# Feed-forward block: the tokens' norm factor behind its first products; attention's first maxima beside the last chain; the queries' weights ahead of the tables

## The reference, cut to what matters

```python
# end of the first block
x = x + y                               # y: the mixed heads times dn_w_out
x = x + squared_relu_mlp(rms_norm(x, norm_mlp[i]), mlp_w_up[i], mlp_w_down[i])
def squared_relu_mlp(h, w_up, w_down):  # D = 1024, D_FF = 4096
    return jnp.square(jax.nn.relu(h @ w_up)) @ w_down
def rms_norm(x, w):                     # y * w, with y = x * rsqrt(mean(x * x) + eps)
...
# second block, attention
qx = apply_rope(rmsnorm(heads(px[0], ATT_HEADS, ATT_HEAD_DIM), g_q[l]), cos, sin)
kx = apply_rope(rmsnorm(heads(px[1], ATT_KV_HEADS, ATT_HEAD_DIM), g_k[l]), cos, sin)
s = jnp.einsum('bqkgd,bnkd->bkgqn', q, keys).astype(jnp.float32) * scale
p = jax.nn.softmax(s, axis=-1)
```

## Time and profile before

| | |
|---|---|
| median of 3 runs | 3222.49 us (3222.05 to 3223.61) |
| profiled execution: time, span | 3223.74 us, 3222.0 us |
| PE busy | 3057.1 us, 95% of the span |
| DVE, ACT, POOL busy | 1556.7, 997.9, 450.8 us |
| mean granted clock of TensorE | 0.982 |
| chain that ended last, PE's share | 85% |

### The profile page before, as it was taken

One profiled execution on the slowest core, in us unless ns is written; L12 is line 12 of the kernel. 1 busy time (PEld: TensorE's weight loads), 2 busy tenths in 40 slices (PEclk: granted clock), 3 DMA queues, 4 the chain that ended last, 5 costly groups with the idle time before them and its releaser, 6 DMA issues.

```text
span 3222.0 us, 36124 instructions
## 1 busy us (share of the span) xinstructions
PE 3057.1 (95%) x14927; PEld 2493.4 (77%) x14927; DVE 1556.7 (48%) x1915; ACT 997.9 (31%) x1440; POOL 450.8 (14%) x352
## 2 busy tenths in 40 slices
PE   7899999989899999999979999999998999999997
PEld 5688888878688888888765667888876888888886
DVE  7566666653565553433456773466654222222224
ACT  5555555552211122212333332233232211111111
POOL 4333333321000001001300000233310000000001
PEclk9999999999999999999989999999999999999999
DMA  3111111122133431111220001011131111111111
GB/s 123 40 47 47 46 47 46 47 66 98 59 118 118 128 117 57 47 52 46 92 54 5 9 9 44 20 40 34 53 107 31 52 53 46 46 52 46 46 46 59
DMA packets 77236, 184.76 MB, mean 57 GB/s; under 512 B 7056, under 2 KB 29072, under 8 KB 77072
## 3 DMA queue, kind: packets, MB, share of 16 engines
q1 hardware_dynamic: 77072, 182.44, 17.9%
HBM read 163.87 MB, written 15.79 MB: 56 GB/s over the span
## 4 chain that ended last, share of the span: by engine, by line
PE 85%; DVE 8%; ACT 4%; issue 2%; DMA 0%; POOL 0%; SPq 0%; POOLq 0%; DVEq 0%; ACTq 0%
PE ps L512 38%; PE ps L1561 18%; PE ps L2886 9%; PE ps L2227 4%; DVE b L2835 2%; PE ps L2365 1%; PE ps L2195 1%; PE ps L909 1%; PE ps L2220 1%; PE ps L2219 1%; DVE b L501 1%; ACT b L493 1%; PE ps L916 1%; PE ps L86 1%; PE ps L891 1%
## 5 line engine op out<-in xcount | busy, mean ns | idle before, releaser
L512 PE MATMUL ps<-b 128*128 128x512 f32 x6024 | 1498.5, 400 | 40.1 <-DVE b L501 13.6
L512 PEld LDWEIGHTS ps<-b 128*128 128x128 f32 x6024 | 1111.2, 190 | 258.2 <-issue 19.2
L1561 PE MATMUL ps<-b 128*128 128x512 f32 x2592 | 599.1, 392 | 0.7 <-DVE b L1696 0.7
L1561 PEld LDWEIGHTS ps<-b 128*128 128x128 f32 x2592 | 485.1, 188 | 109.2 <-DVE b L1696 1.1
L501 DVE TENSOR_TENSOR b<-b 128x1024 fp32r<-128x1024 f32 (+1 forms) x206 | 255.4, 1241 | 298.8 <-ACT b L493 291.9
L493 ACT ACTIVATE b<-b 128x1024 fp32r<-128x1024 f32 (+1 forms) x206 | 215.1, 1045 | 524.5 <-PE ps L1561 427.6
L2886 PE MATMUL ps<-b 128*128 128x512 f32 (+1 forms) x1464 | 330.1, 381 | 6.8 <-ACT b L2946 5.9
L2886 PEld LDWEIGHTS ps<-b 128*128 128x128 f32 x1464 | 257.1, 193 | 57.0 <-issue 11.6
L1610 ACT ACTIVATE b<-ps 128x1024 f32<-128x1024 f32 x54 | 55.4, 1026 | 378.4 <-PE ps L512 378.4
L1400 POOL TENSOR_TENSOR b<-b 128x1024 f32<-128x1024 f32 x18 | 43.2, 2399 | 915.5 <-ACT b L1431 915.1
L2227 PE MATMUL ps<-b 128*128 128x512 f32 x320 | 162.9, 592 | 0.0
(11 more groups left out here) (304 smaller groups left out, 3287.9 us busy)
## 6 DMA issues: line engine op xcount, KB each, us to landing
b<-in_down SPq DMA_DIRECT2D x52, 512.0 KB, 3.6
b<-in_mod SPq DMA_DIRECT2D x96, 256.0 KB, 2.6
b<-in_gu SPq DMA_DIRECT2D x44, 512.0 KB, 3.6
b<-scratch SPq DMA_DIRECT2D x38, 512.0 KB, 4.4
b<-in_dn_in SPq DMA_DIRECT2D x32, 512.0 KB, 4.9
b<-in_up SPq DMA_DIRECT2D x32, 512.0 KB, 3.7
b<-in_win SPq DMA_DIRECT2D x26, 512.0 KB, 3.7
scratch<-b SPq DMA_DIRECT2D x18, 512.0 KB, 2.9
```

The costliest lines, as they stand in the source:

```text
L512: ins = e.matmul(ps[:, c], w, h[:, k, c], start=first and k == 0 and i == 0, stop=last and k == KT - 1 and i == 2)
L1561: ins = e.matmul(ps[:, c], w, u[:, at[k], c], start=k == 0 and p == 0, stop=k == n - 1 and p == 2)
```

## The change

There are four edits.

1. **The tokens' factor moves.** relu(r h) is r relu(h) for r > 0. So x times the column weight alone goes into the first feed-forward block's products. The high and low parts of tiles 0 to 6 are made during the last projection unit, as soon as TensorE has left each tile (event "taken"), and of tile 7 behind the last addition. TensorE does unit 0, then the column sums, then unit 1, then the turn into rows; ScalarE copies the rows to SBUF (`row`). In the body VectorE does relu and the factor in one instruction on the bank, and ScalarE squares. The bank is given back by VectorE's event. ScalarE, VectorE and TensorE no longer wait for each other in `after_project` here; SP does.
2. **The first turn's maxima.** `after_qkv` goes from TensorE and VectorE; in its place stand waits for what each instruction reads. The four maxima of turn 0 go to two sets of banks in turns.
3. **The weight unit at index win 4 + 4** (win 3, for queries) is asked for behind the stores of x, ahead of the two tables.
4. **Memory.** The context's squares and sum use the modulation's buffers, which are free by then; `row`, `amax` and `aneg` get places.

```diff
@@ memory
-            self.c_sq = [sb([128, TC], ctx=ph) for _ in range(2)]
-            self.c_acc = sb([128, TC], ctx=ph)
+            self.c_sq, self.c_acc = [b[:, 0:TC] for b in self.mraw], self.macc[0][:, 0:TC]
+            self.m1["row"] = sb([128, T], ctx=ph)
@@ pe_project
+                if name == "dn_out" and i == KT - 1 and k < KT - 1:
+                    ins.then_inc(*P.up("taken", k))
...
         if name == "w_out":
             e.wait_ge(*V.at("first", KT - 1))
-        self.pe_stat(e, m, sig, "p")
+            self.pe_stat(e, m, sig, "p")
@@ act_project
+        first = name == "dn_out"
+        for k in range(KT - 1 if first else 0):
+            e.wait_ge(*P.at("taken", k))
+            self.act_plain(e, m, sig, k)
         e.wait_ge(*V.at("add", KT - 1))
+        if first:
+            e.wait_ge(*self.gm.at(j0 + KT - 1))
+            self.act_plain(e, m, sig, KT - 1)
         self.act_stat(e, m, sig, "p", KT - 1, m["x"][:, KT - 1, :])
-        self.after_project(e, sig)
+        if not first:
+            self.after_project(e, sig)
+    def act_plain(self, e, m, sig, k):
+        e.activation(self.b_hi[:, k, :], m["x"][:, k, :], ACT.Copy,
+                     scale=self.par("norm_mlp")[:, k:k + 1]).then_inc(*sig[1].up("h", k))
+    def dve_plain(self, e, m, sig, k):
+        e.wait_ge(*sig[1].at("h", k))
+        e.scalar_tensor_tensor(out=self.b_lo[:, k, :], in0=m["x"][:, k, :], scalar=self.par("norm_mlp")[:, k:k + 1],
+                               in1=self.b_hi[:, k, :].bitcast(F32), op0=ALU.mult, op1=ALU.subtract).then_inc(*sig[2].up("l", k))
@@ dve_project
+            elif i == KT - 1:
+                for k in range(KT - 1):
+                    self.dve_plain(e, m, sig, k)
...
+        if gate is None:
+            self.dve_plain(e, m, sig, KT - 1)
+        else:
+            self.after_project(e, sig)
@@ mlp_slots
-            slots[0:2] = [(1, ("act", 0)), (1, ("act", 1))]
+            slots = [(2, ("relu", event[1])) if event[0] == "act" else (engine, event) for engine, event in slots]
@@ pe_mlp (the gated block keeps the old order)
+        else:
+            for i in range(2):
+                e.wait_ge(*self.ww.at(j0 + i))
+                e.wait_ge(*V.at("add", KT - 2 + i))
+                for k in range(KT):
+                    e.wait_ge(*V.at("l", k))
+                    for part in range(2):
+                        ins = self.gemm_piece(e, self.psl[i], j0 + i, k, part, self.b_hi, self.b_lo)
+                ins.then_inc(*self.gm.up(j0 + i))
+                if i == 0:
+                    self.pe_stat(e, m, sig, "p")
+            tokens()
...
+            elif not gated:
+                e.wait_ge(*A.at("row"))
@@ act_mlp
+        if shift is None:
+            e.wait_ge(*P.at("rw"))
+            e.activation(m["row"], self.psl[2], ACT.Copy).then_inc(*A.up("row"))
...
+                    e.wait_ge(*V.at("relu", f))
+                    e.activation(b, b, ACT.Square).then_inc(*A.up("act", f))
+                    e.wait_ge(*A.last())
@@ dve_mlp
-        e.wait_ge(*P.at("rw"))
-        for k in range(KT):
+        e.wait_ge(*P.at("rw") if gated else A.at("row"))
+        for k in range(KT if gated else 0):
...
-                    e.tensor_tensor(b, b, b, ALU.mult).then_inc(*V.up("mul", f))
+                    e.wait_ge(*self.gm.at(ja))
+                    if f >= 2:
+                        e.wait_ge(*V.at("ul", f - 2))
+                    e.scalar_tensor_tensor(out=b, in0=self.psl[self.slot_of(n_ff, ring, gated, f)], scalar=0.0, in1=m["row"],
+                                           op0=ALU.max, op1=ALU.mult).then_inc(*V.up("relu", f))
@@ sp_between
             e.dma_start(self.scratch[1][:, k, :], self.x1[:, k, :]).then_inc(*self.xst.up(k))
+        self.sp_weights(e, UNIT["win", 4] + 5)
@@ pe_qkv, dve_qkv
-        self.after_qkv(e)
@@ pe_attend, maxima(i, j)
+            mx = MX[1 if i else j % 2]
+            if i:
+                e.wait_ge(*(V.at("mx", i, j - 1) if j else V.at("q2", i - 1)))
+            else:
+                n = j + 1
+                if j == 0:
+                    e.wait_ge(*self.aq[1].at("th", 0, "x"))
+                    e.wait_ge(*self.stack[0].at(0, "x", 1))
+                    e.wait_ge(*self.aq[2].at("rp", 3, "x"))
+                elif j == 1:
+                    e.wait_ge(*self.aq[1].at("tv", ("win", 5), 2))
+                else:
+                    e.wait_ge(*V.at("mx", 0, j - 2))
+                e.wait_ge(*self.aq[1].at("th", n, "x"))
+                e.wait_ge(*self.stack[n % 3].at(n, "x", 1))
...
+                if t == 0:
+                    for tag in "cx":
+                        e.wait_ge(*self.aq[2].at("tl", 0, tag))
+                    e.wait_ge(*self.aq[3].at("fill"))
```

More of the change, by code:

```diff
@@ L417, in memory @@
                 self.vx = sb([128, 10, 192], ctx=at, side="right")
+                self.amax, self.aneg = (sb([128, n], ctx=at, side="right") for n in (8, 72))
                 with ExitStack() as tmp:
@@ L428, in memory @@
                 self.arec = sb([128, 512], ctx=at)
-                self.amax, self.aneg = (sb([128, n], ctx=at) for n in (8, 72))
             with ExitStack() as gl:
@@ L1507, in pe_mlp, with tokens @@
         gated = up == "gu"
-        rows_done = V.at("rc")
-        e.wait_ge(*rows_done)
-        rows(e, self.psl[2], self.st[:, 0:8], self.con("ident")).then_inc(*P.up("rw"))
         slots = self.mlp_slots(n_ff, ring, gated)
-        uses = 0
         j0 = UNIT[up, 0]
-        for k in range(KT):
[L1515 to L1522, removed]
+        def tokens():
+            e.wait_ge(*V.at("rc"))
+            rows(e, self.psl[2], self.st[:, 0:8], self.con("ident")).then_inc(*P.up("rw"))
+        if gated:
+            tokens()
[3 more added lines that the diff above has]
+                    for i in range(2):
+                        if k == 0 and part == 0:
+                            e.wait_ge(*self.ww.at(j0 + i))
+                        ins = self.gemm_piece(e, self.psl[i], j0 + i, k, part, self.b_hi, self.b_lo)
+                        if k == KT - 1 and part == 1:
+                            ins.then_inc(*self.gm.up(j0 + i))
+        else:
+            for i in range(2):
+                e.wait_ge(*self.ww.at(j0 + i))
+                e.wait_ge(*V.at("add", KT - 2 + i))
+                for k in range(KT):
+                    e.wait_ge(*V.at("l", k))
+                    for part in range(2):
+                        ins = self.gemm_piece(e, self.psl[i], j0 + i, k, part, self.b_hi, self.b_lo)
+                ins.then_inc(*self.gm.up(j0 + i))
+                if i == 0:
+                    self.pe_stat(e, m, sig, "p")
+            tokens()
         j = j0 + 2
@@ L1582, in act_mlp @@
         e.activation(self.st[:, 8:16], self.st[:, 0:8], ACT.Sqrt).then_inc(*A.up("rt"))
[L1583 to L1587, removed]
+        if shift is None:
+            e.wait_ge(*P.at("rw"))
+            e.activation(m["row"], self.psl[2], ACT.Copy).then_inc(*A.up("row"))
+        else:
+            for k in range(KT):
+                e.wait_ge(*V.at("z", k))
                 e.activation(self.b_hi[:, k, :], m["sq"][k % 2], ACT.Identity, bias=shift[:, k:k + 1]).then_inc(*A.up("h", k))
@@ L1603, in act_mlp @@
                         self.act_weights(e, ja + 3)
-                e.wait_ge(*self.gm.at(ja))
                 b = m["sq"][f % 2]
-                if f >= 2:
-                    e.wait_ge(*V.at("ul", f - 2))
-                else:
[L1609 to L1613, removed]
+                if gated:
+                    e.wait_ge(*self.gm.at(ja))
+                    if f >= 2:
+                        e.wait_ge(*V.at("ul", f - 2))
+                    else:
+                        e.wait_ge(*V.at("l", KT - 1))
+                    e.activation(b, self.psl[self.slot_of(n_ff, ring, gated, f)], ACT.Silu).then_inc(*A.up("act", f))
+                    if f:
+                        self.act_weights(e, ja + 4)
+                    e.wait_ge(*V.at("mul", f))
+                else:
+                    e.wait_ge(*V.at("relu", f))
+                    e.activation(b, b, ACT.Square).then_inc(*A.up("act", f))
+                    e.wait_ge(*A.last())
                 if f >= ring:
@@ L1666, in dve_mlp @@
             e.wait_ge(*A.at("h", k))
[L1667 to L1672, removed]
+            e.scalar_tensor_tensor(out=self.b_lo[:, k, :], in0=z, scalar=shift[:, k:k + 1],
+                                   in1=self.b_hi[:, k, :].bitcast(F32), op0=ALU.add, op1=ALU.subtract).then_inc(*V.up("l", k))
         j = j0 + 2
@@ L2158, in attend_banks @@
         ps = self.ps
-        return (ps[:, 0:TA], ps[:, TA:TA + 128], [ps[:, 1536 + 512 * i:2048 + 512 * i] for i in range(3)],
+        return ([ps[:, 1536:1536 + TA], ps[:, 0:TA]], ps[:, TA:TA + 128], [ps[:, 1536 + 512 * i:2048 + 512 * i] for i in range(3)],
                 [ps[:, 3072:3584], ps[:, 3584:4096]])
@@ L2189, in maxima @@
```

(12 more changed lines are left out.)

6 lines of the change are left out of this document (2 added, 4 removed).

## The result

The changed kernel takes 3190.44 us in the median of 4 runs (3189.41 to 3190.96), the one before 3223.05 on the same chip (3222.05 to 3225.42): the ratio is 0.9896 with a 95% interval of 0.9883 to 0.9908. That is 32.6 us less; 29.5 less was forecast, 3193.0, in a range of 3186 to 3201.

A forecast was written before the change was run, and what follows sets the result against it. TensorE, busy 95% of the span, was taken as the bound, so only its waits and slow-clock time could be won. 10.8 - 0.1 + 9.7 + 9.1 = 29.5 us off the 3222.49 median gave 3193.0, range 3186 to 3201.

The forecast's parts named there:

- Part one: Start of the first feed-forward block: factor applied behind relu, unit 4 ends sooner; gain 10.8 us, bounds 7.8 and 14.2.
- cover for tile 7: First feed-forward block's start: tile 7 ready at 818.2, wanted by TensorE at 823.1, so 4.9 us to spare.
- the slow clock behind it comes back: Units 3 and 4, behind a wait of 5.1 us: 96 passes run partly at slow clock again, 25.2 us.
- my bound of 14.2: First feed-forward block's start: the gain in us if there is no slow stretch at all.
- Part two: Body of the first feed-forward block: relu and square trade engines, hidden except in the last group; loss 0.1 us.
- Part three: Queries' weights ahead of the tables: wait of 5.83 us goes, slow clock behind it returns 3.9; gain 9.7.
- Part four: First maxima beside the last chain: three rounds of 3.02 us gone; gain 9.1, lower bound 6.0.
- The waits go, the slow clock does not: Rival at TensorE's joints: waits vanish but half clock stays; gain 22.6 us, 3199.9; chance 0.16.
- The slow stretches go altogether: Rival at TensorE's joints: no slow-clock stretches remain; gain 36.5 us, 3186.0; chance 0.12.
- The lost start: Rival at first feed-forward block's start: modulation's loads hold unit 3, no gain there; 18.7 us in all, 3203.8; chance 0.07.
- the slower case: Rival in the block's body: VectorE gives up banks too late; at 12.5 us a unit, 3244; chance 0.02.
- the null: Rival for the whole kernel: change does nothing within 0.2% (6.4 us), each wait replaced by an equal one; chance 0.02.

The follow-up runs named there:

- e1_first: Changed kernel without the early load of the queries' weight unit and with attention as before; median 3211.89 us, ratio 0.9964 to the kernel before.
- e10_late_parts: Changed kernel with high and low parts of tiles 0 to 6 made behind the last projection unit; stage to unit 4's end 140.8 us, against 135.1.
- e4_early: Changed kernel with unit 3's high and low weights made ahead of the row copy; median 3184.95 us, ratio 0.9878 to the kernel before.
- e2_load: Kernel before with only the early load of the queries' weight unit; median 3214.11 us, ratio 0.9968.
- e3_maxima: Kernel before with only the first turn's maxima beside the last chain; median 3216.04 us, ratio 0.9976.
- e8_between: Changed kernel with the queries' weight unit asked for between the two table loads; span 3200.5 us, against 3189.1.
- e9_ahead: Changed kernel with the queries' weight unit asked for just ahead of both tables, not 20 us earlier; span 3196.8 us, against 3189.1.
- e6_onebank: Changed kernel with the first turn's four maxima in one bank set, no common barrier; turn of values to second turn's first maximum 17.25 us, against 13.28.
- e7_barrier: Changed kernel with the common barrier back on TensorE and VectorE, two bank sets kept; turn of values to second turn's first maximum 18.19 us, against 13.28.
- e5_mid: e4_early with the turn into rows put inside unit 1, ahead of its tile 5; median 3186.01 us.
- e11_early_again: e4_early run once more, unchanged; median 3183.46 us.
- e12_mid_again: e5_mid run once more, unchanged; median 3184.81 us.

## Why the prediction was right

**What bounds the kernel.** Right. Of the 32.9 us between the spans 31.6 lie at the three joints where TensorE waited or ran at half clock; the long stretches of products behind the first and the last of them stayed at 658.3 and 250 us.

**Part one, 10.8 forecast, 12.5 measured.** The mechanism and the order of events came as written: tile 7 was ready ahead of its turn (VectorE's parts end at 817.4, TensorE wants tile 7 near 821), the waits were 1.21 and 4.71 for a forecast of 1.1 and 5.1. The cover for tile 7 was 3.5 us, not 4.9: the last addition stood behind the low parts of the tiles before on VectorE, until 813.7, 2.2 us behind the projection's last pass and not 1.0. In the sum for unit 3 the rows give 0.1 + 1.1 = 1.2 more for the chain, where the working has 1.1; it is too small to matter. The mis-sized term is "the slow clock behind it comes back": I gave it 3.4 us (25.2 for 96 passes) and it was 1.9 (23.64). Its size isn't fixed by the wait: behind the same wait of 4.71 the runs show 1.7 (e1_first), 1.9 and 3.0 (e10_late_parts). So that it was 1.9 and not 3 in the changed kernel's profile is partly luck. That the stage can have no slow stretch at all, my bound of 14.2 at this place, was shown by e4_early, where the wait is gone too.

**Part two, +0.1 forecast, 0.0 measured.** The body took 658.31 in both. The group rows of the page after, VectorE's relu and ScalarE's square:

```profile
L1661 ACT ACTIVATE b<-b 128x1024 f32<-128x1024 f32 x32 | 33.9, 1060 | 251.8 <-DVE b L1741 251.8
...
L1741 DVE SCALAR_TENSOR_TENSOR b<-ps,b 128x1024 f32<-128x1024 f32 x32 | 39.2, 1224 | 148.1 <-PE ps L512 135.9
```

VectorE's instruction from PSUM took 1.224, not the 1.275 of the earlier trace rows, so the pair is 0.04 longer than before and not 0.09: 1.22 + 1.06 for 1.02 + 1.22. By the Trainium skill's table (VectorE: DVE Perf Modes, The TRN2 errata) it would be 0.11 dearer by my estimate; the trace agrees for ScalarE's half (1.06 from SBUF, 1.02 from PSUM) and not for VectorE's (1.22 either way). Nothing hung on it: TensorE never waited for a relu.

**Part three, 9.7 forecast, 9.9 measured** up to the second head-norm sums. Both halves, the wait of 5.83 and the slow passes behind it, went, in e2_load as in the changed kernel. Against the same stage in e3_maxima and e1_first the gain would be 10.3 and 11.2. e8_between and e9_ahead show that the place in the queue and the earliness both count. The 1.6 in the stage behind it was not forecast, and e2_load takes it away from this edit: that stage took from 64.5 to 69.4 us with the same passes, and what picks the length is open.

**Part four, 9.1 forecast, 9.2 measured.** Maximum 3 starts behind the copy as the working has it, and the three others are ahead of it; e6_onebank and e7_barrier split it into 5.2 and 4.3.

**The rivals.** "The waits go, the slow clock does not" fell: from the 18 passes to the second sums the clock stayed at 1.00, in the changed kernel as in e2_load. "The slow stretches go altogether" did not come; there was less of them than forecast (23.64 us for 96 passes, where the full clock gives 21.8). The lost start, the slower case and the null did not come.

**What makes up the 3.1 between forecast and result.** 1.7 from part one (1.6 of it slow passes of units 3 and 4), 1.6 from the chains' stage, 0.2 and 0.1 from parts three and four, 0.1 from the body: 3.7 in spans at the joints. Stages whose code is unchanged moved by -2.0, +2.2, -0.3 and +0.4, which is 0.3 in sum. The rest is that spans of one execution are compared here and medians above. That so little is left is luck too: the moves of unchanged stages happen to cancel, and in e6_onebank the chains' stage took 4.8 us more than in the changed kernel, with no instruction ahead of its end changed. The +2.2 in the linear recurrence stands in nine of the eleven profiles with the first edit (434.7 to 435.4), while before, e2_load and e3_maxima have 432.6, 432.5 and 433.2; but e6_onebank and e7_barrier, with the first edit in, have 433.2 and 433.1. In e1_first and e4_early one of eight equal windows of it has clock 0.94, where before has 0.97 at the lowest. Whether an edit leads to it, and by what, is open; no run was made for it.

## What to carry to other kernels

At a joint between stages, a wait of the bounding engine can cost more than its length: price it with the slow passes that can follow (nothing was lost behind waits of 1.21 us, up to 3.3 behind 2.83), and look for idle time of the helper engines just ahead of it into which late work can go (e4_early: two calls, 6.6 us in the stage). A factor that commutes with the next product can be applied behind it, and then the statistics stop being a barrier. Where a stage is entered through a common barrier, ask what each first instruction really reads; here more buffers and fewer waits each gave about half.

## What the runs showed of the hardware that was not expected

Unchanged code takes different times, and TensorE's clock has a part in it. The stage of the chains, with the same passes, took 64.5 us in three profiles (changed, e1_first, e7_barrier), 66.0 to 66.1 in seven (before, e3_maxima, e4_early, e8_between, e9_ahead, e10_late_parts, e11_early_again) and 69.2 to 69.4 in four (e2_load, e5_mid, e6_onebank, e12_mid_again). Its mean granted clock was 0.95, 0.92 and 0.90 in the three groups, with two exceptions: e1_first took 64.5 at 0.92, and e3_maxima 66.1 at 0.95. So the mean clock alone doesn't give the length; where the slow stretches fall seems to count too, which no run separates.

The edit isn't what picks the length. The changed kernel, e6_onebank and e7_barrier have the same instructions up to the end of this stage, and took 64.5, 69.2 and 64.5. Two kernels that were profiled twice each did fall on the same length both times, which may be chance; what picks it is open. An edit of 1.4 us ahead of the stage can thus disappear in it (e5_mid's profiles).

How long a slow stretch lasts isn't given by the wait ahead of it: 1.7 to 3.0 us lost behind 4.71 us of waiting, 3.0 behind 3.57 (before), 3.3 behind 2.83 (17.1 for 13.8 in e9_ahead). Here too the same instructions differ. In the changed kernel the 96 passes of units 3 and 4 took 23.64, in e6_onebank a microsecond more:

```profile
854.30 24.62 PE L512 MATMUL ps<-b 128*128 128x512 f32 x96 [4.71 <-DVE b L501]
```
